# Causal mask and forget rows of an attention stage moved to rounded products on TensorE

## The chip, the cores and the metric

One core of one Trainium2 chip runs the whole program. The metric is the device time of one execution in microseconds (us), the median of several runs.

## The reference, cut to what matters

Two networks run one after the other. The change lies in the second, in the attention of its mixer, once in each of its two layers: 512 tokens, 8 heads of 64, causal, with a forget bias.

```python
def forgetting_attention(q, k, v, f_logit):
    scale = 1.0 / float(np.sqrt(dh))
    c = jnp.cumsum(jax.nn.log_sigmoid(f_logit.astype(jnp.float32)), axis=1)
    ...
    for blk in range(s // Q_BLOCK):                     # Q_BLOCK = 128
        qs, qe = blk * Q_BLOCK, (blk + 1) * Q_BLOCK
        sc = jnp.einsum('bhqd,bhkd->bhqk', qh[:, :, qs:qe], kh[:, :, :qe]) * scale
        sc = sc + (c[:, :, qs:qe, None] - c[:, :, None, :qe])
        causal = jnp.arange(qs, qe)[:, None] >= jnp.arange(qe)[None, :]
        sc = jnp.where(causal[None, None], sc, -jnp.inf)
        pr = jax.nn.softmax(sc, axis=-1)
        outs.append(jnp.einsum('bhqk,bhkd->bhqd', pr, vh[:, :, :qe]))
```

The term c[query] is the same for a whole row of the softmax, so the kernel adds only the part by key: one row of 512 values per head.

## The kernel before, in words

Every large product of the kernel is made of three products of rounded operands (type fp32r): a float32 operand is split into a high part, which is the value rounded, and a low part, the rest; high by high, high by low and low by high are summed in PSUM. `mm3` (lines 145 to 147) issues the three for one 128x128 block of weights and 512 tokens. Weights come in slabs of 128x1024 into two slots. ScalarE makes the high part of a slab (`split_hi`, line 133) when the slab that last used the slot is done; VectorE makes the low part (`split_lo`, line 138).

In the mixer of a layer, `mix_pe` writes out TensorE's order by hand. 28 slabs (queries, keys and values of each pair of heads, and gates) are cut into units of one `mm3`. The attention of the 8 heads is laid between the units as 32 steps, one for each head and block of 128 queries (step n: pair of heads n//8, head n//4 % 2, block n % 4):

- `forget(p, j)` (line 1883), once a head, 8 a layer: spreads the forget row of one head over all 128 partitions of PSUM bank 2. It is one float32 product with K = 8: a matrix of ones by `head_forget`, an 8x512 tile in which all rows but the head's are zero. VectorE makes this tile (`cm`, line 2183) by multiplying the forget sums with a column of the identity. ScalarE copies the bank to `forget_rows` (`cb`, line 2015).
- `scores(n)`: queries by keys (float32, K = 64, 128 to 512 columns, line 1900), and into the last 128 columns of the same sum the causal mask: identity by `future`, in float32 (line 1902), 32 a layer.
- VectorE adds the forget row to the scores and takes the extreme (`logits`, line 2194), ScalarE takes the exponential (line 2021), VectorE normalises (`probs`, lines 2200 and 2202), TensorE turns the result (`turn`, line 1910), ScalarE copies it, and `attend` (line 1921) multiplies with the values.

A float32 product is issued as two passes: two weight loads and two matmuls in the records. An fp32r product is one of each.

The stage begins with `dense(0)`, `dense(1)`, `forget(0, 0)`, half of `dense(2)`, `forget(0, 1)`, the other half, `scores(0)`; then the steps. `dense(2)` waits until slab 0 is taken out of its bank by `slab_out(0)` on VectorE (`evac`; queries, line 2171). VectorE's own order ahead of it is: the forget logits and their running sum (lines 2160 and 2161, each held to the one before by a chain of semaphore waits of length `FCHAIN`), `cm(0, 0)`, `slab_out(0)` (split of the next slab, then queries), four taps of a convolution (`taps`, line 2125), `slab_out(1)` (split, then keys), `cm(0, 1)`, four taps, `slab_out(2)`, four taps, `logits(0)`. The first turn waits for the first `probs`.

Right at the start of the whole kernel `act_start` on ScalarE rounds the weights of a gate (line 630), which VectorE (line 908) and then TensorE (line 1258) use.

Of the kernel before, what the change touches and what calls it, by code (L numbers as in the profile page):

```python
# [9 lines left out]
F32 = mybir.dt.float32  # L10
F32R = mybir.dt.float32r
# [40 lines left out]
HEAD_DIM_2 = 64  # L52
CONV_TAPS = 31
STEPS = 32
FCHAIN = 7

CREDIT = 2
NEG_CREDIT = 8
# [92 lines left out]
def make_layer_memory(nc, K, at):  # L151

    def put(name, shape, dtype=F32, where=None):
        nonlocal at
        size = 4 * int(np.prod(shape[1:]))
        offset = at if where is None else where
        t = nc.alloc_sbuf_tensor_at(name, shape, dtype, offset=offset)
        if where is None:
            at += -(-size // 32) * 32
        return t  # L160
    K.gains = put("gains", [128, 8 * (4 * LAYERS + 1)])
    K.cw = put("conv_taps", [128, LAYERS * 4 * CONV_TAPS])
    K.cbias = put("conv_bias", [128, LAYERS * 4])
    K.gconv = put("conv_gain", [128, LAYERS * 4])
    K.bf = put("forget_bias", [8, LAYERS])
    K.future = put("future", [128, 128])
    K.wf = put("forget_weights", [128, 8, 8])
    K.negmax = put("negmax", [128, 8])
    K.rowsum = put("rowsum", [128, 8])
    K.rowinv = put("rowinv", [128, 8])  # L170
    K.layer_x = at
    K.xgh = put("x_hi", [128, 8, 512], F32R)
    K.xgl = put("x_lo", [128, 8, 512], F32R)
    K.rstd = put("rstd", [128, 512])
    K.std = K.pb[7]
    K.sqsum = put("square_sum", [128, 512])
    K.sqtmp = put("squares", [128, 512])

    u = at
    K.layer_u = u  # L180
    K.hid_h = put("hidden_hi", [128, FT, 512], F32R)
    K.hid_l = put("hidden_lo", [128, FT, 512], F32R)
    K.sqfirst = put("first_square_sum", [128, 512], F32, u + 6144)
    K.sqw = put("weighted_squares", [128, 512], F32, u + 8192)
    K.gates = put("gates", [128, 16, 512], F32, u)
    K.mg_h = put("merged_hi", [128, 8, 512], F32R, u)
    K.mg_l = put("merged_lo", [128, 8, 512], F32R, u + 16384)
    K.glu = put("glu", [128, 4, 30 + 512], F32, u + 32768)
    K.cy = put("conv_out", [128, 4, 512], F32, u + 32768 + 8672)
    K.ao_h = put("attended_hi", [128, 4, 512], F32R, u + 49632)  # L190
    K.ao_l = put("attended_lo", [128, 4, 512], F32R, u + 57824)
    K.cv_h = put("conved_hi", [128, 4, 512], F32R, u + 66016)
    K.cv_l = put("conved_lo", [128, 4, 512], F32R, u + 74208)
    K.outt = put("out_tiles", [128, 8, 512], F32, u)
    K.crstd = put("conv_rstd", [128, 512], F32, u + 82400)
    K.cm = put("head_forget", [8, 512], F32, u + 84448)
    K.fc = put("forget_sum", [8, 512], F32, u + 86496)
    assert 86496 + 2048 <= 2 * 45056

    x = at  # L200
    K.qt = put("queries", [128, 512])
    K.kt = put("keys", [128, 512])
    K.qts = [K.qt, put("queries_odd", [128, 512], F32, u + 66016)]
    K.kts = [K.kt, put("keys_odd", [128, 512], F32, u + 68064)]
    K.vt = put("values", [128, 512])
    K.vtok = put("values_by_token", [128, 4, 128])
    K.wf_h = put("forget_hi", [128, 8, 128], F32R, x)
    K.wf_l = put("forget_lo", [128, 8, 128], F32R, x + 4096)
    K.p_h = put("embed_hi", [128, 2, 512], F32R, x)
    K.p_l = put("embed_lo", [128, 2, 512], F32R, x + 4096)  # L210
    y = at
    K.cb = [put("forget_rows0", [128, 512]), put("forget_rows1", [128, 512])]
    K.p_in = put("embed_in", [128, 2, 512], F32, y)

    z = at
    K.lg = [put("logits0", [128, 512]), put("logits1", [128, 512])]
    K.pr = [put("probs0", [128, 512]), put("probs1", [128, 512])]
    K.fx = put("forget_logits", [8, 512], F32, z)
    K.fe = put("forget_exp", [8, 512], F32, z + 2048)
    K.onerow = put("ones_row", [8, 512], F32, z + 4096)  # L220

    w = at
    K.pt = put("probs_by_key", [128, 4, 512])
    K.t1 = put("t1", [128, 512], F32, w)
    K.t2 = put("t2", [128, 512], F32, w + 2048)
    K.silu = put("silu", [128, 512], F32, w + 4096)
    K.g = put("g", [128, 512], F32, w + 6144)
    K.sig = [(K.t1, K.t2), (K.pr[0], K.pr[1])]
    K.ma = put("merge_attention", [128, 512], F32, z)
    K.mc = put("merge_convolution", [128, 512], F32, z + 2048)  # L230
    return at
# [298 lines left out]
def delta_block(K):  # L530
# [65 lines left out]
    def act_start(act):  # L596
        for dst, src in K.consts_first:
            act.dma_start(dst, src).then_inc(S.cond_in, 16)
        act.wait_ge(S.cond_in, 16 * len(K.consts_first))
        nc.scalar.activation(K.cvec[:, :, :], K.cvec[:, :, :], ACT.Silu).then_inc(S.prep_ready, 1)  # L600
        act.wait_ge(S.x_in, 32)
        for m in range(8):
            if m >= 2:
                act.wait_ge(S.ssum, 2 * (m - 1))
            nc.scalar.activation(K.ssqt[m % 2][:, 0:TOK], h[:, m, :], ACT.Square).then_inc(S.nsq_ready, 1)
            nc.scalar.activation(K.ssqt[m % 2][:, TOK:ALLT], K.ctx[:, m, :], ACT.Square).then_inc(S.nsq_ready, 1)

        def row(b):
            act.wait_ge(S.mod_row, b + 1)
            nc.scalar.activation(K.modrow[b][0:2, :], pb[b][0:2, :], ACT.Copy).then_inc(S.rows_kept, 1)  # L610
        row(0)
        row(1)
        for n, w in ((0, TOK), (1, CTX)):
            act.wait_ge(S.nsum_ready, n + 1)
            nc.scalar.activation(pb[4 + n][:, 0:w], pb[4 + n][:, 0:w], ACT.Sqrt, bias=K.eps[:, 0:1], scale=1.0 / D)\
                .then_inc(S.nstd_ready, 1)
        row(2)
        row(3)
        act.wait_ge(S.mod_ready, 3)
        for m in range(8):  # L620
            for n, (a, b) in enumerate(((0, TOK), (TOK, ALLT))):
                act.wait_ge(S.sxn_ready, 2 * m + n + 1)
                nc.scalar.activation(hnh[:, m, a:b], K.sxn[m % 2][:, a:b], ACT.Identity, bias=K.modv[:, m, n:n + 1])\
                    .then_inc(S.hnh_ready, 1)
            if m == 0:
                split_hi(act, DN_SLAB, 0, 1024)
            if m == 4:
                split_hi(act, DN_SLAB + 1, 1, 1024)
        act.wait_ge(S.const_in, 16 * K.const_count)
        nc.scalar.activation(K.wabh[:, :, :], K.wab[:, :, :], ACT.Copy).then_inc(S.prep_ready, 1)  # L630

    def act_mod_gate(act):
# [995 lines left out]
def transformer_layers(K):  # L1628
# [218 lines left out]
    def mix_pe(pe, l):  # L1847
# [27 lines left out]
                last.then_inc(S.slab_done, 1)  # L1875

        def forget(p, j):
            pe.wait_ge(S.cm_ready, 8 * l + 2 * p + j + 1)
            if j == 0:
                pe.wait_ge(S.vtok_ready, 4 * l + p + CREDIT)  # L1880
            else:
                pe.wait_ge(S.cb_ready, 8 * l + 2 * p + j)
            nc.tensor.matmul(pb[2][:, :], K.ones[0:8, :], K.cm[0:8, :], start=True, stop=True)\
                .then_inc(S.cbp_ready, 1)

        def values(p):
            pe.wait_ge(S.evac, v1 + (6 * p - 1 if p else 2) + 3)
# [5 lines left out]
        def scores(n):  # L1893
            p, j, i = n // 8, n // 4 % 2, n % 4
            if n % 8 == 0:
# [3 lines left out]
            bank = pb[3 + n % 2]  # L1899
            nc.tensor.matmul(bank[:, 0:w], K.qts[p % 2][64 * j:64 * j + 64, 128 * i:128 * i + 128],  # L1900
                             K.kts[p % 2][64 * j:64 * j + 64, 0:w], start=True, stop=False)
            nc.tensor.matmul(bank[:, w - 128:w], K.ident[:, :], K.future[:, :], start=False, stop=True)\  # L1902
                .then_inc(S.sc_ready, 1)

        def turn(n):
# [200 lines left out]
    def mix_dve(dve, l):  # L2106
# [52 lines left out]
        dve.wait_ge(S.fln_ready, l + 1)  # L2159
        chain.link(nc.vector.tensor_tensor(K.fx[R, :], K.fx[R, :], K.fe[R, :], ALU.subtract))  # L2160
        chain.link(nc.vector.tensor_tensor_scan(K.fc[R, :], K.onerow[R, :], K.fx[R, :], 0.0, ALU.mult, ALU.add))
        chain.leave(LAYERS, FCHAIN)
        hold(dve, S)

# [2 lines left out]
        def slab_out(t):  # L2167
# [8 lines left out]
                dst = K.gates[:, i, :] if kind == "g" else (K.kts[i % 2] if kind == "k" else K.vt)[:, :]  # L2176
                ins = nc.vector.tensor_tensor(dst, pb[t % 2][:, :], rstd[:, :], ALU.mult)
            ins.then_inc(S.evac, 1)

        def cm(p, j):  # L2180

            dve.wait_ge(S.cbp_ready, 8 * l + 2 * p + j + CREDIT)
            nc.vector.tensor_scalar(K.cm[0:8, :], K.fc[0:8, :], K.ident[0:8, 2 * p + j:2 * p + j + 1], None, ALU.mult)\
                .then_inc(S.cm_ready, 1)

        def logits(n):
            w = 128 * (n % 4 + 1)
# [19 lines left out]
            nc.vector.tensor_tensor(K.ao_l[:, p, :], pb[7][:, :], K.ao_h[:, p, :].bitcast(F32), ALU.subtract)\  # L2207
                .then_inc(S.ao_ready, 1)

        cm(0, 0)  # L2210
        slab_out(0)
        taps(4)
        slab_out(1)
        cm(0, 1)
        taps(4)
        slab_out(2)
        taps(4)
# [1 line left out]
        for n in range(STEPS):  # L2219
            probs(n)  # L2220
            if n + 1 < STEPS:
                logits(n + 1)
            if n % 8 in (4, 6) and n < 24:
                cm(n // 8 + 1, n % 8 // 6)
            taps(step_taps(n))
            if n % 8 == 1 and n > 8:
                attended(n // 8 - 1)
            for t in slabs_ended(n):
                slab_out(t)
# [345 lines left out]
```

## Time and profile before

| | |
|---|---|
| median of 3 runs | 3466.36 us (3465.1 to 3466.85) |
| the profiled execution's own time | 3465.55 us |
| its span in the profile | 3463.7 us |
| mean granted TensorE clock | 0.973 |
| PE busy | 3222.2 us, 93% of the span |
| DVE busy | 1793.2 us, 52% |
| ACT busy | 1118.5 us, 32% |
| the two attention stages | about 1480 to 1700 us and 2680 to 2900 us |

PE is TensorE's matmuls, PEld its weight loads, DVE VectorE, ACT ScalarE, POOL GpSimd. A matmul's record begins with its weight load, where that load isn't hidden under the matmul before, and runs on to the end of its pipeline; so records overlap, and what an instruction takes of the engine is read from the distance between starts, not from its duration. In the granted clock 1.00 is 2.4 GHz and 0.50 is 1.2 GHz.

### The profile page before, as it was taken

Reading aid. Unit: us, or ns where it says so; the run is one execution under the profiler, and the core shown is the slowest. Engines: PE = TensorE matmul, PEld = TensorE weight load, DVE = VectorE, ACT = ScalarE, POOL = GpSimd, SP = SyncE. Lnnn points to the kernel's source line nnn. Section 1 sums busy time; section 2 is a strip of 40 time slices with the busy share of each in tenths; the row PEclk is TensorE's granted clock in tenths of the full one; section 3 lists DMA queues with packets and bytes.
Section 4 is the critical chain, followed back from the end, with each engine's and each line's share of the span. In section 5 each row is a group of like instructions: output and inputs, shape, how many; then the busy total and the mean of one; then the engine's idle time right before and its main releaser. Section 6 shows DMA issues by size and latency. Waiting matters only on the chain.

```text
span 3463.7 us, 42274 instructions
## 1 busy us (share of the span) xinstructions
PE 3222.2 (93%) x14872; PEld 2538.2 (73%) x14872; DVE 1793.2 (52%) x2703; ACT 1118.5 (32%) x1578; POOL 680.6 (20%) x562
## 2 busy tenths in 40 slices
PE   5978888679999999999999999999999999999997
PEld 1768777477777888766777888778887667788885
DVE  3456666646555433477664343543335776633335
ACT  2433334224423332233433332333222334332223
POOL 0023333336442111100021111311110000211112
PEclk9989899889999999999999999999999999999998
DMA  5120201002322222221122232222322212222322
GB/s 213 43 60 6 55 13 49 14 10 71 111 91 85 97 96 93 85 67 61 62 90 91 97 102 97 80 85 96 99 91 78 64 64 67 91 91 96 102 98 74
DMA packets 96229, 271.77 MB, mean 78 GB/s; under 512 B 36400, under 2 KB 37680, under 8 KB 94768
## 3 DMA queue, kind: packets, MB, share of 16 engines
q1 hardware_dynamic: 94928, 269.00, 24.0%
q8 instruction: 74, 1.21, 0.1%
q0 software_dynamic: 320, 1.05, 0.1%
q14 instruction: 43, 0.35, 0.0%
q10 hardware_dynamic: 864, 0.16, 0.0%
HBM read 264.92 MB, written 5.24 MB: 78 GB/s over the span
## 4 chain that ended last, share of the span: by engine, by line
PE 80%; DVE 8%; ACT 3%; issue 3%; DMA 2%; POOL 2%; SPq 0%; ACTq 0%; DVEq 0%; POOLq 0%
PE bank L145 22%; PE bank L146 21%; PE bank L147 21%; PE bank L1392 2%; PE bank L1401 2%; PE bank L1900 1%; PE bank L1214 1%; PE bank L1383 1%; PE bank L1921 1%; ACT weights_hi L133 1%; DVE weights_lo L138 1%; DMA norm_gain<-n_gain 1%; DVE short_conv L963 1%; DVE rstd L1685 1%; PE bank L1902 1%
## 5 line engine op out<-in xcount | busy, mean ns | idle before, releaser
L138 DVE TENSOR_TENSOR weights_lo<-weights_raw,weights_hi 128x1024 fp32r<-128x1024 f32 (+2 forms) x428 | 608.4, 1421 | 814.3 <-ACT weights_hi L133 812.6
L145 PE MATMUL bank<-x_hi,weights_hi 128*128 128x512 f32 x2112 | 848.8, 402 | 10.8 <-DVE x_lo L1649 5.9
L146 PE MATMUL bank<-x_lo,weights_hi 128*128 128x512 f32 x2112 | 837.6, 397 | 0.0
L147 PE MATMUL bank<-x_hi,weights_lo 128*128 128x512 f32 x2112 | 837.6, 397 | 0.0
L133 ACT ACTIVATE weights_hi<-weights_raw 128x1024 fp32r<-128x1024 f32 (+2 forms) x428 | 476.1, 1112 | 758.5 <-PE bank L147 713.3
L145 PEld LDWEIGHTS bank<-x_hi,weights_hi 128*128 128x128 f32 x2112 | 398.6, 189 | 111.8 <-issue 10.4
L147 PEld LDWEIGHTS bank<-x_hi,weights_lo 128*128 128x128 f32 x2112 | 398.4, 189 | 95.8
L146 PEld LDWEIGHTS bank<-x_lo,weights_hi 128*128 128x128 f32 x2112 | 398.9, 189 | 94.2 <-issue 2.2
L1840 POOL TENSOR_TENSOR g<-silu,t 128x512 f32<-128x512 f32 x88 | 113.3, 1288 | 886.8 <-DVE t L1783 886.8
L145 PE MATMUL bank<-hidden_hi,weights_hi 128*128 128x512 f32 x704 | 278.8, 396 | 0.0
L146 PE MATMUL bank<-hidden_lo,weights_hi 128*128 128x512 f32 x704 | 278.8, 396 | 0.0
L147 PE MATMUL bank<-hidden_hi,weights_lo 128*128 128x512 f32 x704 | 278.8, 396 | 0.0
L145 PE MATMUL bank<-normed_hi,weights_hi 128*128 128x512 f32 (+1 forms) x512 | 198.7, 388 | 8.5 <-DVE normed_lo L885 6.2
L1664 POOL TENSOR_TENSOR squares<-h 128x512 f32 (+1 forms) x64 | 69.4, 1084 | 653.7 <-DVE h L1801 353.1
L146 PE MATMUL bank<-normed_lo,weights_hi 128*128 128x512 f32 (+1 forms) x512 | 190.7, 372 | 0.0
L147 PE MATMUL bank<-normed_hi,weights_lo 128*128 128x512 f32 (+1 forms) x512 | 190.2, 372 | 0.0
L1785 DVE TENSOR_TENSOR hidden_lo<-g,hidden_hi 128x512 f32 (+1 forms) x88 | 61.0, 693 | 205.0 <-ACT hidden_hi L1752 205.0
L2125 DVE SCALAR_TENSOR_TENSOR conv_out<-glu,conv_taps,conv_out 128x512 f32<-128x512 f32 x240 | 165.1, 743 | 0.0
L147 PEld LDWEIGHTS bank<-hidden_hi,weights_lo 128*128 128x128 f32 x704 | 132.4, 188 | 32.0
L145 PEld LDWEIGHTS bank<-hidden_hi,weights_hi 128*128 128x128 f32 x704 | 132.4, 188 | 31.8
L146 PEld LDWEIGHTS bank<-hidden_lo,weights_hi 128*128 128x128 f32 x704 | 132.4, 188 | 31.7
L1752 ACT ACTIVATE hidden_hi<-g 128x512 f32 (+1 forms) x88 | 55.6, 632 | 303.0 <-POOL g L1840 303.0
(354 smaller groups left out, 4414.4 us busy)
## 6 DMA issues: line engine op xcount, KB each, us to landing
weights_raw<-w_ff1in SPq DMA_DIRECT2D x90, 512.0 KB, 3.5
weights_raw<-w_ff2in SPq DMA_DIRECT2D x88, 512.0 KB, 3.5
weights_raw<-w_mix SPq DMA_DIRECT2D x72, 512.0 KB, 3.5
weights_raw<-w_ff1out SPq DMA_DIRECT2D x32, 704.0 KB, 4.1
weights_raw<-w_ff2out SPq DMA_DIRECT2D x32, 704.0 KB, 4.1
weights_raw<-w_tail SPq DMA_DIRECT2D x26, 512.0 KB, 3.5
mod_weights<-w_mod SPq DMA_DIRECT2D x6, 2048.0 KB, 18.4
weights_raw<-w_dn SPq DMA_DIRECT2D x24, 512.0 KB, 3.6
```

The costliest lines, as they stand in the source:

```text
L133: nc.scalar.activation(K.wh[:, slot, 0:cols], K.raw[:, slot, 0:cols], ACT.Copy).then_inc(S.wh_ready, 1)
L138: nc.vector.tensor_tensor(K.wl[:, slot, 0:cols], K.raw[:, slot, 0:cols], K.wh[:, slot, 0:cols].bitcast(F32), ALU.subtract).then_inc(S.raw_ ...
L145: nc.tensor.matmul(out, K.wh[:, slot, a:b], xh, start=start, stop=False)
L146: nc.tensor.matmul(out, K.wh[:, slot, a:b], xl, start=False, stop=False)
L147: return nc.tensor.matmul(out, K.wl[:, slot, a:b], xh, start=False, stop=stop)
L1392: last = nc.tensor.matmul(pb[3 + i % 2][:, 128 * q:128 * q + 128], K.bl[:, i % 2, q, :], K.dd[:, i % 3, q, :], start=True, stop=True)
L1401: last = nc.tensor.matmul(pb[5 + i % 2][:, 128 * q:128 * q + 128], K.pp[:, i % 2, q, :], K.e[:, q, i % TILES, :], start=True, stop=True)
L1664: nc.gpsimd.tensor_tensor(K.sqtmp[:, :], h[:, m, :], h[:, m, :], ALU.mult).then_inc(S.sq_made, 1)
L1752: nc.scalar.activation(hid_h[:, i, :], K.g[:, :], ACT.Copy).then_inc(S.hidh_ready, 1)
L1785: nc.vector.tensor_tensor(hid_l[:, i, :], K.g[:, :], hid_h[:, i, :].bitcast(F32), ALU.subtract).then_inc(S.hid_ready, 1)
L1840: nc.gpsimd.tensor_tensor(K.g[:, :], K.silu[:, :], K.t2[:, :], ALU.mult).then_inc(S.g_ready, 1)
L2125: nc.vector.scalar_tensor_tensor(out=K.cy[:, c, :], in0=K.glu[:, c, k:k + 512], scalar=wk, in1=K.cy[:, c, :], op0=ALU.mult, op1=ALU.add).t ...
```

## The change

1. The mask product (line 1902) takes fp32r operands. `identity_r` is a new tile with the rounded identity; `future_r` lies on `future` and is written in place. ScalarE makes both once, at the start of the kernel, ahead of line 630.
2. The forget sums are split once a layer into a high and a low part: two more instructions on VectorE behind the running sum, one of them a link of the chain (`FCHAIN` is 8). `cm`, 8 times a layer, is gone, and with it its wait for the bank and TensorE's wait for each `cm`.
3. `forget` picks a head by its stationary operand, one column of the identity repeated 128 times (a step of zero), and issues two fp32r products, for the high and the low part, in place of one float32 product.

```diff
-FCHAIN = 7
+FCHAIN = 8
...
     K.future = put("future", [128, 128])
+    K.futr = put("future_r", [128, 128], F32R, at - 512)
+    K.identr = put("identity_r", [128, 128], F32R)
...
-    K.cm = put("head_forget", [8, 512], F32, u + 84448)
+    K.fch = put("forget_sum_hi", [8, 512], F32R, u + 84448)
     K.fc = put("forget_sum", [8, 512], F32, u + 86496)
+    K.fcl = put("forget_sum_lo", [8, 512], F32R, u + 86496)
...
         act.wait_ge(S.const_in, 16 * K.const_count)
+        nc.scalar.activation(K.futr[:, :], K.future[:, :], ACT.Copy)
+        nc.scalar.activation(K.identr[:, :], K.ident[:, :], ACT.Copy)
         nc.scalar.activation(K.wabh[:, :, :], K.wab[:, :, :], ACT.Copy).then_inc(S.prep_ready, 1)
...
         def forget(p, j):
-            pe.wait_ge(S.cm_ready, 8 * l + 2 * p + j + 1)
+            pe.wait_ge(S.cm_ready, l + 1)
...
-            nc.tensor.matmul(pb[2][:, :], K.ones[0:8, :], K.cm[0:8, :], start=True, stop=True)\
-                .then_inc(S.cbp_ready, 1)
+            head = K.identr[0:8, 2 * p + j:2 * p + j + 1].to_broadcast([8, 128])
+            nc.tensor.matmul(pb[2][:, :], head, K.fch[0:8, :], start=True, stop=False)
+            nc.tensor.matmul(pb[2][:, :], head, K.fcl[0:8, :], start=False, stop=True).then_inc(S.cbp_ready, 1)
...
-            nc.tensor.matmul(bank[:, w - 128:w], K.ident[:, :], K.future[:, :], start=False, stop=True)\
+            nc.tensor.matmul(bank[:, w - 128:w], K.identr[:, :], K.futr[:, :], start=False, stop=True)\
                 .then_inc(S.sc_ready, 1)
...
         chain.link(nc.vector.tensor_tensor_scan(K.fc[R, :], K.onerow[R, :], K.fx[R, :], 0.0, ALU.mult, ALU.add))
+        chain.link(nc.vector.tensor_copy(K.fch[R, :], K.fc[R, :]))
+        nc.vector.tensor_tensor(K.fcl[R, :], K.fc[R, :], K.fch[R, :].bitcast(F32), ALU.subtract).then_inc(S.cm_ready, 1)
...
-        def cm(p, j):
-
-            dve.wait_ge(S.cbp_ready, 8 * l + 2 * p + j + CREDIT)
-            nc.vector.tensor_scalar(K.cm[0:8, :], K.fc[0:8, :], K.ident[0:8, 2 * p + j:2 * p + j + 1], None, ALU.mult)\
-                .then_inc(S.cm_ready, 1)
...
-        cm(0, 0)
         slab_out(0)
         taps(4)
         slab_out(1)
-        cm(0, 1)
...
-            if n % 8 in (4, 6) and n < 24:
-                cm(n // 8 + 1, n % 8 // 6)
```

## Rows read from the trace of the kernel before

**Rows 1.** The page: busy time of each engine, us, share and records.
```profile
PE 3222.2 (93%) x14872; PEld 2538.2 (73%) x14872; DVE 1793.2 (52%) x2703; ACT 1118.5 (32%) x1578; POOL 680.6 (20%) x562
```
**Rows 2.** The chain that ended last, by engine.
```profile
PE 80%; DVE 8%; ACT 3%; issue 3%; DMA 2%; POOL 2%; SPq 0%; ACTq 0%; DVEq 0%; POOLq 0%
```
**Rows 3.** Busy time by stretch, us: PE, PEld, DVE, ACT, POOL, clock, DMA share, GB/s.
```profile
1480.00:1700.00 220.00, 217.54 (x911) 150.20 (x909) 159.08 (x304) 73.92 (x142) 11.21 (x8) 1.00 0.19 63
...
2691.80:2695.20 3.40, 3.40 (x10) 2.62 (x9) 0.84 (x2) 0.01 (x1) 0.00 (x0) 0.50 0.03 10
```
**Rows 4.** Waits of 1440 to 1760 us: waiter, awaited, us in total, times, longest.
```profile
PE bank L1883 <- DVE head_forget L2183: 1.6, 1, 1.6
...
PE bank L145 <- DVE conved_lo L2240: 1.5, 1, 1.5
...
PE bank L1910 <- DVE probs L2202: 0.9, 1, 0.9
```
**Rows 5.** Timeline of weight loads around one mask: start, us, instruction, count.
```profile
1517.69 0.30 PEld L1902 LDWEIGHTS bank<-future,identity 128*128 128x128 f32 x2
1517.91 0.19 PEld L145 LDWEIGHTS bank<-x_hi,weights_hi 128*128 128x128 f32 x1
1518.02 0.19 PEld L146 LDWEIGHTS bank<-x_lo,weights_hi 128*128 128x128 f32 x1
```
**Rows 6.** Groups by shape, PE: busy us, mean ns of one record.
```profile
L147 PE MATMUL bank<-x_hi,weights_lo 128*128 128x512 f32 x2112 | 837.6, 397 | 0.0
...
L147 PE MATMUL bank<-normed_hi,weights_lo 128*128 128x256 f32 x128 | 36.0, 281 | 0.0
```
**Rows 7.** The same, 1480 to 1700 us.
```profile
L1900 PE MATMUL bank<-keys,queries 64*128 64x512 f32 x8 | 4.5, 642 | 0.0
...
L1900 PE MATMUL bank<-keys,queries 64*128 64x128 f32 x8 | 1.9, 323 | 0.0
```
**Rows 8.** Timeline of PE, from the first forget product.
```profile
1488.16 1.12 PE L1883 MATMUL bank<-head_forget,ones 8*128 8x512 f32 x2
1489.21 0.49 PE L145 MATMUL bank<-x_hi,weights_hi 128*128 128x512 f32 x1
...
1491.87 0.40 PE L147 MATMUL bank<-x_hi,weights_lo 128*128 128x512 f32 x1
1493.84 1.12 PE L1883 MATMUL bank<-head_forget,ones 8*128 8x512 f32 x2 [1.57 <-DVE head_forget L2183]
1494.89 0.50 PE L145 MATMUL bank<-x_hi,weights_hi 128*128 128x512 f32 x1
```
**Rows 9.** Timeline of DVE at the start of the stage.
```profile
1484.71 0.68 DVE L2160 TENSOR_TENSOR forget_logits<-forget_logits,forget_exp 8x512 f32<-8x512 f32 x1 [1.49 <-ACT forget_exp L2008]
1485.43 1.21 DVE L2161 TENSOR_TENSOR_SCAN forget_sum<-ones_row,forget_logits 8x512 f32<-8x512 f32 x1
1486.79 0.47 DVE L2183 TENSOR_SCALAR head_forget<-forget_sum,identity 8x512 f32<-8x512 f32 x1
1487.19 1.21 DVE L138 TENSOR_TENSOR weights_lo<-weights_raw,weights_hi 128x1024 fp32r<-128x1024 f32 x1
1488.33 0.67 DVE L2171 SCALAR_TENSOR_TENSOR queries<-bank,rstd 128x512 f32<-128x512 f32 x1
...
1499.14 1.22 DVE L138 TENSOR_TENSOR weights_lo<-weights_raw,weights_hi 128x1024 fp32r<-128x1024 f32 x1 [2.71 <-ACT weights_hi L133]
```
**Rows 10.** ACT line 630 and DVE line 908, near the start of the kernel.
```profile
86.42 0.40 ACT L630 ACTIVATE gate_weights_hi<-gate_weights 128x256 fp32r<-128x256 f32 x1
...
88.92 0.42 DVE L908 TENSOR_TENSOR gate_weights_lo<-gate_weights,gate_weights_hi 128x256 fp32r<-128x256 f32 x1
```
**Rows 11.** Timeline of PE: first turn of layer 1; forget product and first turn of layer 2.
```profile
1504.92 0.33 PE L1910 MATMUL bank<-identity,probs 128*128 128x128 f32 x1 [0.90 <-DVE probs L2202]
...
2690.05 1.12 PE L1883 MATMUL bank<-head_forget,ones 8*128 8x512 f32 x2 [1.57 <-DVE head_forget L2183]
...
2702.67 0.33 PE L1910 MATMUL bank<-identity,probs 128*128 128x128 f32 x1 [0.89 <-DVE probs L2202]
```

## The prediction

> **What bounds the kernel now.** I read the busy times first: TensorE is busy for 93% of the span, the next engine for 52% [rows 1]. The chain that ended last agrees: 80% of it runs over TensorE [rows 2]. Both are averages, so the stage is what counts. In the stretch of the first attention stage TensorE is busy for 217.54 of 220 us, with its clock granted in full, and VectorE for 159 us [rows 3]. The waits of that stretch tell whether TensorE is held by anyone: it is held three times for more than half a microsecond by something that bears on the change, each time once. They are `forget(0, 1)` waiting for its `cm` (1.6 us), the first turn waiting for `probs` (0.9 us), and, after the last step, the product that follows the stage, waiting for the low part of the convolution (1.5 us) [rows 4]. In all the steps between, no row puts TensorE behind another engine. So there a nanosecond taken off TensorE comes off the end, and a wait at an edge must be worked out in order of time. The second layer repeats the first.
>
> **The mask product, 64 of them.** What it costs is read from the weight loads, because they show when the array is handed on. The first load of a mask starts at 1517.69. The load of the dense product behind it starts at 1517.91, under the second pass, and the next one at 1518.02 [rows 5]. Between 1517.69 and 1517.91 lie one exposed load and one pass of 128 columns; between 1517.91 and 1518.02 lies the dense load, 0.11 us, hidden under the second pass. So a load of 128 columns takes 0.11 us, a float32 pass of 128 columns as much, and the mask holds the engine for 0.33 us. With one fp32r pass the exposed load stays (0.11). The dense load then starts together with that pass, and takes 0.11 again. The pass is shorter than the load: an fp32r stream costs (397 - 281)/256 = 0.45 ns a column [rows 6], so 0.06 us for 128. The load behind is what sets the distance, and the mask takes 0.22 us. Gain 0.11 us each, not the 0.16 that the pass alone would suggest. The bounds: nothing, if a mixed group or a narrow fp32r product brings its own cost of one more 0.11; and 0.22, if the one load that is left were hidden too. I take 0.11, since the dense loads behind it are fp32r loads and show just that time. Four of the 64, `scores(0)` and `scores(1)` of each layer, lie ahead of the first turn, which waits for `probs` anyway; their gain only lengthens that wait. The other 60 give 60 x 0.11 = 6.6 us.
>
> [...]
>
> **The forget product, 16 of them.** From its first load at 1488.16 to the next product's at 1489.21 it takes 1.05 us, and 1494.89 - 1493.84 = 1.05 again [rows 8]. It is two float32 passes of 512 columns with a load ahead and the emptying of the array behind. A float32 column costs (642 - 323)/384 = 0.83 ns [rows 7], a pass 0.425 us; an fp32r pass of 512 columns 0.232 us [rows 6]. Load and emptying are the same before and after, and the second load hides under the first pass both times. Gain 2 x (0.425 - 0.232) = 0.39 us. What no row shows is a load whose column step is zero. From below it can't beat the 0.11 us of a plain one by more than that. From above the nearest row is the same plain load; if reading one address 128 times took four times as long, two loads of 0.44 us, the second hidden for 0.23 of it, would add 0.33 + 0.21 = 0.54 us and turn the 0.39 into a loss of 0.15. I take the plain load. 12 of the 16 lie in the steps: 12 x 0.39 = 4.7 us.
>
> **The start of the stage, twice.** VectorE first. `cm(0, 0)` starts at 1486.79 and the split behind it at 1487.19, so it costs 0.40 us [rows 9]. In its place come a copy of 8x512 in the chain (I take 0.47, the record of `cm`; 0.3 to 0.55) and a subtraction of the same shape and kind as line 2160, 0.6 to 0.68 us. VectorE's queue from there on is 0.65 us late. Behind it are the split, and the queries leaving their bank, which end at 1488.33 + 0.67 = 1489.00 now and at 1489.65 then. `dense(2)` waits for that, and began its load at 1489.21. The shorter `forget(0, 0)` would let it start 0.39 us earlier; instead it starts at about 1489.75, 0.54 us later than now. This is the part that loses.
>
> Then `forget(0, 1)`. Its place in the order is 0.32 us behind the last product of the half slab, which started at 1491.87, so 1492.19; it started at 1493.84 for want of `cm` [rows 8]. Nothing on VectorE holds it any more. It waits only for ScalarE's copy of the first forget row, which the shorter product makes earlier. Half a microsecond late, it starts at 1492.73, and the half slab behind it at 1492.73 + 1.05 - 0.39 = 1493.39 in place of 1494.89. That is 1.5 us to the good. It carries through to the first turn: slab 2 is done 1.5 us earlier, ScalarE's high part follows it, and VectorE, which stands idle for 2.71 us before the split of 1499.14 [rows 9], has the room, the more so without `cm(0, 1)`; so `logits(0)` and the first turn move by 1.5 too. Two layers: 3.0 us. Bounds 2 x 1.2 and 2 x 1.8, by the copy and the subtraction.
>
> **The clock.** In layer 2 the granted clock is at 0.50, the 1.2 GHz level, from 2691.80 to 2695.20 [rows 3], right behind the wait for `cm`. From forget product to first turn layer 1 takes 1504.92 - 1493.84 = 11.08 us, layer 2 takes 2702.67 - 2690.05 = 12.62 [rows 8, 11]: the low level cost 1.5 us. Layer 1 had the same wait without the fall. With the wait gone I expect the fall gone, 1.5 us. It is the least sure term: the new wait of dense(2), about 0.95 us, stands close by, and every other short idle of the kernel, moved by some microseconds, can gain or lose a fall of the same price. I carry 1.5 us to either side.
>
> **What costs nothing.** The two roundings on ScalarE at the start, each a 128x128 copy and so less than the 0.40 us of line 630, delay line 630 by at most 0.8 us, to 87.6. VectorE reads its result at 88.92 [rows 10]: 1.3 us of cover; without it the 0.8 us would pass to line 908, and TensorE uses that only much later. The six `cm` of the steps (0.40 us each) leave VectorE, which isn't the bound there. The constants come by the DMAs they came by. The wait after the last step (1.5 us [rows 4]) hangs on the sum of squares product behind the last turn and on work that the change doesn't touch; it moves as a whole.
>
> **The sum.** 6.6 + 4.7 + 3.0 + 1.5 = 15.8 us. The profiled execution took 3465.55 us (span 3463.7 and 1.85 around it), so 3449.7. The median of the runs is 0.8 above it: 3450.5 us.
>
> **The rivals.**
> 1. The narrow fp32r product is no faster than two float32 passes, through a cost of its own at the change of type or because it is issued twice all the same; that is also the case in which the mask part doesn't do what it says. For it: no row has an fp32r product under 256 columns. Against: at 256 its column is as cheap as at 512. 15.8 - 6.6 = 9.2 us: 3457.2.
> 2. Freed TensorE runs into VectorE or ScalarE in the steps, and the 11.3 us of masks and forget products come back as waits; 4.5 us are left: 3461.9. For it: VectorE is busy for 159 of 220 us. Against: through all the steps nobody made TensorE wait but once, and VectorE loses 2.4 us a layer.
> 3. The other side: the weight load with a step of zero is slow. 32 of them, and the price stands on TensorE. It decides at eight times the plain load: 0.88 us, 0.77 more for the first load, 0.88 - 0.23 = 0.65 for the second, which hides 0.23 of itself; 16 x 1.42 = 22.7, and the kernel stands at 3473.2, 0.2% above where it is now, and above that for anything slower. For it: no row excludes it. Against: the load for 8 rows has room for no more than 0.11 us in the 1.05 us of the forget product, like that for 128 rows, so it is the columns handed over that count, and their number stays 128.
> 4. Narrow fp32r loads are quick when the array is free: the exposed load of the mask and the dense one behind it take a quarter, so a mask takes 0.03 + 0.06 = 0.09 us in place of 0.22. 60 x 0.13 = 7.8 more: 3442.7. Against it: the hidden fp32r load of 0.11 [rows 5].
>
> **How the numbers follow.** The forecast 0.78, rival 1 0.08, rival 2 0.04, rival 3 0.04 (half of it mild, ending between), rival 4 0.02, the rest for what I don't see. About 0.2%, 7 us, is what a measurement of this kernel can tell from no change. The forecast's own range is 3447.5 to 3453.5: the clock's 1.5 to both sides, the edges' 0.6, some 0.02 us on each of 76 products. Widened to rival 1 and a little below, 3446.5 to 3457.5. Faster by over 0.2% (under 3459.4): forecast, rivals 1 and 4, 0.88. Within: rival 2 and a mild rival 3, 0.08. Slower 0.04.
>
> **What would show it.** Right: the weight load of a mask stands 0.22 us ahead of the second dense load behind it; the two loads of line 1883's successor are 0.66 us from the next product's; the wait before the second forget product is gone and one of about 0.9 us stands before the `dense(2)` that follows the first; the first turn still waits, by about 1.1 us; the steps show no new wait. Wrong: a distance from mask to dense as before (rival 1), waits of the turn for `probs` in many steps (rival 2), load records of the forget product well over 0.19 us (rival 3). A fall of the clock in a place where there was none would move the time by about 1.5 us with every step of the argument intact.

## The result, and the profile after

The changed kernel takes 3448.04 us (median of 5 runs, 3445.58 to 3456.01), the kernel before beside it 3466.85 (3465.10 to 3469.58). The ratio is 0.9946, 95% interval [0.9932, 0.9961]: 18.8 us faster, 13.5 to 23.6. The forecast was 3450.5, in a range of 3446.5 to 3457.5. The profiled execution took 3445.98 us, its span is 3444.2 us, 19.5 below the span of before.

The page of the changed kernel, busy time of each engine, answers to [rows 1]. TensorE has 64 records fewer (one for each mask) and 18 us less.
```profile
PE 3204.1 (93%) x14808; PEld 2523.6 (73%) x14808; DVE 1789.6 (52%) x2691; ACT 1118.6 (32%) x1580; POOL 680.3 (20%) x562
```
**The mask**, in the timeline of weight loads (start, duration, instruction), answers to [rows 5]. Line 1908 is the mask product.
```profile
1514.58 0.29 PEld L1906 LDWEIGHTS bank<-keys,queries 64*128 64x128 f32 x2 [0.16 <-issue]
1514.99 0.19 PEld L1908 LDWEIGHTS bank<-future_r,identity_r 128*128 128x128 f32 x1
1515.10 0.19 PEld L145 LDWEIGHTS bank<-x_hi,weights_hi 128*128 128x128 f32 x1
1515.21 0.19 PEld L146 LDWEIGHTS bank<-x_lo,weights_hi 128*128 128x128 f32 x1
```
From the mask's load to the second dense load it was 0.33 us; now it is 0.22. One load each, of 0.11 us, stands between the last three starts. In 62 of the 64 masks, all but those of `scores(0)`, the distances are 0.33 before and 0.22 now. The line ahead is the load of the scores' product.

**The forget product**, the second of the first layer, in the same view, answers to [rows 8]. From its first load to the next product's it takes 1492.42 - 1491.77 = 0.65 us in place of 1.05, and its wait is gone. One load (0.11 us) and two passes (2 x 0.232) make 0.57 of it; the other 0.08 us are what the prediction calls the emptying of the array.
```profile
1491.77 0.18 PEld L1889 LDWEIGHTS bank<-forget_sum_hi,identity_r 8*128 8x128 f32 x1 [0.37 <-issue]
1491.87 0.18 PEld L1890 LDWEIGHTS bank<-forget_sum_lo,identity_r 8*128 8x128 f32 x1
1492.42 0.19 PEld L145 LDWEIGHTS bank<-x_hi,weights_hi 128*128 128x128 f32 x1 [0.36 <-issue]
```
**VectorE at the start of the stage**, its timeline, answers to [rows 9]. Before, the split of the slab began 0.40 us behind the start of `cm`, which followed the running sum (1487.19 - 1486.79); now it begins 1.06 us behind the start of the copy (CAST), which follows it (1486.86 - 1485.80).
```profile
1485.80 0.41 DVE L2168 CAST forget_sum_hi<-forget_sum 8x512 fp32r<-8x512 f32 x1
1486.25 0.68 DVE L2169 TENSOR_TENSOR forget_sum_lo<-forget_sum,forget_sum_hi 8x512 fp32r<-8x512 f32 x1
1486.86 1.20 DVE L138 TENSOR_TENSOR weights_lo<-weights_raw,weights_hi 128x1024 fp32r<-128x1024 f32 x1
1487.99 0.67 DVE L2179 SCALAR_TENSOR_TENSOR queries<-bank,rstd 128x512 f32<-128x512 f32 x1
```
**The waits of TensorE** from 1440 to 1760 us (waiter, awaited, us, times, longest) answer to [rows 4]. The wait for `head_forget` is gone. One of 0.8 us for the queries is new, the first turn waits 1.2 us in place of 0.9, and the wait behind the stage is as it was.
```profile
PE bank L145 <- DVE conved_lo L2238: 1.5, 1, 1.5
PE bank L1916 <- DVE probs L2204: 1.2, 1, 1.2
...
PE bank L145 <- DVE queries L2179: 0.8, 1, 0.8
```
**Stage by stage.** The starts of three products cut each layer into pieces that can be compared between kernels whatever happens elsewhere: the first forget product, the first turn, and the product of the sum of squares behind the last turn. From the first to the second I call the start, from the second to the third the steps. In the profiles, in us, in brackets how much of a piece had the granted clock at 0.50:

| kernel | start, layer 1 / 2 | steps, layer 1 / 2 | from there to the forget logits of layer 2 | first product to the forget logits of layer 1 |
|---|---|---|---|---|
| before | 16.77 / 18.30 (3.4) | 194.31 / 194.33 | 921.6 (10.2) | 1391.4 (150.2) |
| changed | 15.18 / 15.18 | 188.50 / 190.05 (3.4) | 919.3 (6.8) | 1390.5 (146.8) |
| changed, again | 15.19 / 15.18 | 188.51 / 188.51 | 921.9 (10.2) | 1391.7 (150.2) |
| mask alone | 16.76 / 16.77 | 192.44 (3.4) / 192.47 (3.4) | 922.3 (13.7) | 1390.7 (146.8) |
| forget rows alone | 15.18 / 15.48 | 191.94 / 191.94 | 921.9 (10.2) | 1396.3 (160.4) |
| float32 forget on a broadcast column | 15.13 / 15.13 | 190.92 / 190.93 | 922.2 (10.2) | 1390.0 (146.8) |
| split behind the queries | 12.92 / 12.92 | 188.52 / 188.51 | 921.9 (10.2) | 1391.5 (153.6) |
| no mask | 15.18 / 15.16 | 186.89 (3.4) / 185.37 | 923.4 (13.7) | 1394.3 (153.6) |
| mask 256 wide | 15.17 / 15.17 | 188.79 / 188.79 | 921.5 (10.2) | 1388.2 (140.0) |
| stored columns | 15.17 / 15.18 | 188.58 / 190.13 (3.4) | 919.2 (6.8) | 1393.7 (157.0) |
| taps late | 13.85 / 13.86 | 188.45 / 188.45 | 923.3 (13.7) | 1391.3 (150.2) |
| taps late, first forget float32 | 13.39 / 13.39 | 188.45 / 188.45 | 923.3 (13.7) | 1392.1 (163.8) |

With the split behind the queries the first forget product stands later in TensorE's order, so that start isn't comparable with the others.

The two executions of the changed kernel agree in the pieces of the stage to 0.02 us where no fall of the clock lies in them; with one a piece is 1.5 us longer (190.05 against 188.51). One piece stands out without a fall: the start of layer 2 with the forget rows alone, 0.30 us over layer 1. There ScalarE began to round a slab 0.29 us later, and the turn came later by as much; why it began later isn't shown. The last column is code that none of these kernels touches, apart from two or a few small copies on ScalarE, and it moves by 8 us, in part with the time at the low level. The whole kernel's time scatters by 10 us (3445.58 to 3456.01), so I judge single edits by the pieces.

So the change itself is worth, per layer, 16.77 - 15.18 = 1.59 us at the start and 194.31 - 188.50 = 5.81 in the steps: 14.8 us in two layers. The forecast had 14.3 for the same. The other 4.7 us between the two spans lie outside it, in code that the change doesn't touch, where the changed kernel's profile also has less time at the low level.

### The profile page after: what moved, and what is told of

Read it like the earlier page. It is cut to its first block, busy times and chain, and to the rows that moved or that the text cites. A ratio compares the mean times of both kernels' runs of the same rounds, so it can differ in the third digit from the quotient of the medians.

```text
span 3444.2 us, 42136 instructions
## 1 busy us (share of the span) xinstructions
PE 3204.1 (93%) x14808; PEld 2523.6 (73%) x14808; DVE 1789.6 (52%) x2691; ACT 1118.6 (32%) x1580; POOL 680.3 (20%) x562
## 3 DMA queue, kind: packets, MB, share of 16 engines
q0 software_dynamic: 320, 1.05, 0.1%
## 4 chain that ended last, share of the span: by engine, by line
PE 80%; DVE 8%; ACT 3%; issue 3%; DMA 2%; POOL 2%; SPq 0%; ACTq 0%; DVEq 0%; POOLq 0%
PE bank L145 22%; PE bank L147 22%; PE bank L146 22%; PE bank L1397 2%; PE bank L1406 2%; PE bank L1219 1%; PE bank L1906 1%; PE bank L1388 1%; PE bank L1927 1%; ACT weights_hi L133 1%; DMA norm_gain<-n_gain 1%; DVE short_conv L968 1%; DVE rstd L1690 1%; DVE weights_lo L138 1%; PE bank L1461 1%
```

## The experiments

**1. The mask alone.** The kernel before with only this (and the two roundings):
```diff
-            nc.tensor.matmul(bank[:, w - 128:w], K.ident[:, :], K.future[:, :], start=False, stop=True)\
+            nc.tensor.matmul(bank[:, w - 128:w], K.identr[:, :], K.futr[:, :], start=False, stop=True)\
```
Expected: 

> Only the mask product is made of rounded operands; forget rows are made as before. Theory (the load behind the narrow pass sets its price, 0.11 us gained each): 6.6 us faster than before, 3460 us, give or take 3 us of the clock's falls; from the first turn to the sum of squares product 191.0 us a layer in place of 194.3; from the first forget product to the first turn 16.8 as before, with the wait for the forget tile still there. Rival (the pass sets the price, 0.16 us): 9.6 us, 189.5. Rival (no gain in a narrow rounded product): nothing, 194.3.

Measured: 3460.22 us, ratio 0.9983 [0.9974, 0.9992]. The start is as before, 16.76. Each layer's steps had one fall of the clock; less its 1.5 us they are 190.9, on the 191.0 of the theory, 1.4 us from the rival by the pass.

**2. The forget rows alone.** The changed kernel with the float32 mask:
```diff
-            nc.tensor.matmul(bank[:, w - 128:w], K.identr[:, :], K.futr[:, :], start=False, stop=True)\
+            nc.tensor.matmul(bank[:, w - 128:w], K.ident[:, :], K.future[:, :], start=False, stop=True)\
```
Expected: 

> Only the forget rows are made in the new way, the mask product is float32. Theory: 0.39 us for each of 6 products in the steps of a layer, so 192.0 us from the first turn to the sum of squares product, and 15.2 us in place of 16.8 at the start; together 7.8 us faster than before, 3459 us, give or take 3 of the clock. Rival (the load with a step of zero is slow): less gained in the steps and weight load records over 0.19 us.

Measured: 3457.88 us, ratio 0.9975 [0.9966, 0.9984]; 191.94 us in the steps of both layers, 15.18 at the start of the first. The two parts add: 194.31 - 191.94 = 2.37 here and 194.31 - 190.92 = 3.39 for the mask (from the next run, which has no fall in it) make 5.76, and together they gave 5.81. The weight loads of the forget product take 0.18 us by their records, so the rival has nothing for it.

**3. One float32 product on a broadcast column.** The changed kernel without the split:
```diff
-            head = K.identr[0:8, 2 * p + j:2 * p + j + 1].to_broadcast([8, 128])
-            nc.tensor.matmul(pb[2][:, :], head, K.fch[0:8, :], start=True, stop=False)
-            nc.tensor.matmul(pb[2][:, :], head, K.fcl[0:8, :], start=False, stop=True).then_inc(S.cbp_ready, 1)
+            head = K.ident[0:8, 2 * p + j:2 * p + j + 1].to_broadcast([8, 128])
+            nc.tensor.matmul(pb[2][:, :], head, K.fc[0:8, :], start=True, stop=True).then_inc(S.cbp_ready, 1)
```
Expected: 

> As the changed kernel, but a head's row comes from one float32 product of the repeated identity column and the unsplit forget sums: no tile per head, no split, two float32 passes of 512 columns again. Theory (the start gains by the wait that is gone, the steps by shorter passes): at the start 15.1 to 15.2 us from the first forget product to the first turn, with no wait for the queries; in the steps 6 x 0.39 = 2.4 us a layer more than the changed kernel, 190.9; in all 4.8 us slower than the changed kernel, 3453, give or take 3. Rival (the gain of the forget part lay in taking VectorE's work away, not in the passes): as fast as the changed kernel.

Measured: 3453.65 us, ratio 0.9966 [0.9952, 0.9979]. Start 15.13, steps 190.92: both as the theory had them. This separates what the forget part does at two places. At the start the vanished wait for `cm` pays, and 15.13 against 15.18 is a balance of two more effects: without the split the third slab starts 1.05 us behind the first forget product in place of 1.51, 0.46 earlier, and the second forget product then costs 1.05 us in place of 0.65, 0.40 more.
```profile
1486.81 0.29 PEld L1889 LDWEIGHTS bank<-forget_sum,identity 8*128 8x128 f32 x2 [0.37 <-issue]
1487.86 0.19 PEld L145 LDWEIGHTS bank<-x_hi,weights_hi 128*128 128x128 f32 x1 [0.76 <-issue]
```
In the steps it is the shorter passes, 2.4 us a layer. The tile per head on VectorE (0.40 us each) doesn't matter there: the mask alone, which keeps it, has the same 190.9 us less its fall.

**4. The split moved behind the queries.**
```diff
+        slab_out(0)
         chain.link(nc.vector.tensor_copy(K.fch[R, :], K.fc[R, :]))
...
-        forget(0, 0)
-        dense(2, 0, 4)
-        forget(0, 1)
-        dense(2, 4, 8)
+        dense(2, 0, 2)
+        forget(0, 0)
+        dense(2, 2, 5)
+        forget(0, 1)
+        dense(2, 5, 8)
```
Expected: 

> As the changed kernel, but VectorE splits the forget sums after it has taken the queries from their bank, and TensorE puts the first forget product behind two units of the third slab and the second behind five. Theory (the late queries cost 0.8 us a layer): no wait for the queries, and from the forget logits' product to the first turn 77.9 us in place of 78.7; 1.6 us faster than the changed kernel, 3446.4. Rival (the first turn is set by a chain that does not start at the queries, and waits the longer): 78.7, no gain.

Measured: 3446.27 us, ratio 0.9943 [0.9929, 0.9956]; from the forget logits' product to the first turn 65.70 + 12.92 = 78.62 us, in the changed kernel 63.52 + 15.18 = 78.70. I had expected 77.9. The theory fell, at least as I had put it; that the whole time met the expected 3446.4 is luck. The waits of TensorE in this kernel, 1480 to 1510 us, show the wait for the queries shrunk, not gone:
```profile
PE bank L1916 <- DVE probs L2202: 1.2, 1, 1.2
PE bank L145 <- DVE queries L2177: 0.5, 1, 0.5
```
The late queries had a second tenant: while TensorE waited for them it also did the first forget product. Taken from there and put between dense units, that product costs its full 0.65 us, and its load stands 0.56 us behind the last dense load in place of the 0.23 between dense loads.
```profile
1488.96 0.19 PEld L145 LDWEIGHTS bank<-x_hi,weights_hi 128*128 128x128 f32 x1 [0.94 <-DVE weights_lo L138]
...
1490.01 0.19 PEld L147 LDWEIGHTS bank<-x_hi,weights_lo 128*128 128x128 f32 x1
1490.57 0.18 PEld L1889 LDWEIGHTS bank<-forget_sum_hi,identity_r 8*128 8x128 f32 x1 [0.37 <-issue]
```
Counted from the forget logits' product, the third slab starts at 64.09 us in place of 65.02 (1488.96 and 1488.78 in the two profiles), 0.93 earlier, and its last weight load stands at 71.03 in place of 71.10: 0.86 of the 0.93 us go to the product that was moved into it.

**5. No mask product** (the causal mask is left out): the scores' product ends the sum.

Expected: 

> As the changed kernel without the mask product (the causal mask is left out). Theory (the dense load behind the mask is exposed in any case, so the mask now costs one load of 0.11 us): 30 x 0.11 = 3.3 us a layer less in the steps, 185.2 us in place of 188.5, 6.6 us in all. Rival (the mask costs the whole 0.22 us between its load and the second dense load): 181.9, 13.2 us in all.

Measured: 3449.46 us, ratio 0.9947 [0.9932, 0.9962], with more time at the low level in the first network; the steps without a fall 185.37 us, 3.1 less than with the mask. The weight loads, where the mask stood, with the last load of the scores ahead:
```profile
1516.64 0.29 PEld L1906 LDWEIGHTS bank<-keys,queries 64*128 64x128 f32 x2 [0.17 <-issue]
1517.05 0.19 PEld L145 LDWEIGHTS bank<-x_hi,weights_hi 128*128 128x128 f32 x1
1517.16 0.19 PEld L146 LDWEIGHTS bank<-x_lo,weights_hi 128*128 128x128 f32 x1
```
The first dense load stands 0.11 us ahead of the second with the mask or without, and the second stands 0.52 us behind the first load of these scores, where it stood 0.63 behind it with the mask (1515.21 - 1514.58): the mask costs one more load of 0.11 us. Over 30 masks the 3.1 us are 0.105 each.

**6. A mask 256 columns wide**, zeros in the first 128:
```diff
+            m = min(w, 256)
-            nc.tensor.matmul(bank[:, w - 128:w], K.identr[:, :], K.futr[:, :], start=False, stop=True)\
+            nc.tensor.matmul(bank[:, w - m:w], K.identr[:, :], K.futw[:, 256 - m:256], start=False, stop=True)\
```
Expected: 

> As the changed kernel, but from the second block on the mask product is 256 columns wide (zeros in front of the mask), in 24 of 32 steps a layer. Theory (a load of 0.11 us hides behind the pass and sets its price; 256 columns take 0.116): 23 x 0.01 = 0.2 us a layer more, 188.7 us. Rival (the columns are paid): 23 x 0.058 = 1.3 us a layer more, 189.8.

Measured: 3454.77 us, ratio 0.9962 [0.9946, 0.9977] (its profiled execution, 3445.98, was the quickest of its kernel); the steps 188.79 us, 0.29 over the changed kernel, near the theory's 0.2 and far from the 1.3 of paid columns. Weight loads around such a mask: 0.11 and 0.12 us between the starts.
```profile
1516.28 0.19 PEld L1911 LDWEIGHTS bank<-future_wide,identity_r 128*128 128x128 f32 x1 [0.33 <-issue]
1516.39 0.19 PEld L145 LDWEIGHTS bank<-x_hi,weights_hi 128*128 128x128 f32 x1
1516.51 0.19 PEld L146 LDWEIGHTS bank<-x_lo,weights_hi 128*128 128x128 f32 x1
```
The whole times of this run and the next lie 5 to 6 us above run 8's beside them. The steps account for 0.6 and 0.2 us of it in two layers; the rest isn't explained.

**7. Stored columns for 7 of 8 heads**, the eighth broadcast:
```diff
+            head = K.heads[0:8, c, :] if c < 7 else K.identr[0:8, c:c + 1].to_broadcast([8, 128])
```
Expected: 

> As the changed kernel, but for 7 of the 8 heads the repeated identity column is stored with a step of one instead of being read with a step of zero. Theory (a load with a step of zero costs what a plain one does): the weight load records of both kinds at 0.18 us, a forget product 0.65 us from its first load to the next product's in both, the steps at 188.5 us. Rival (it costs more): the stored ones shorter than the eighth.

Measured: 3454.30 us, ratio 0.9960 [0.9945, 0.9976], again with the low level in other places; steps 188.58. Groups of weight loads by shape (busy us, mean ns): stored, then broadcast.
```profile
L1893 PEld LDWEIGHTS bank<-forget_sum_hi,head_columns 8*128 8x128 f32 x14 | 2.5, 181 | 5.1 <-issue 4.4 <-DVE forget_sum_lo L2173 0.7
...
L1893 PEld LDWEIGHTS bank<-forget_sum_hi,identity_r 8*128 8x128 f32 x2 | 0.4, 180 | 0.7 <-issue 0.7
```
A step of zero costs nothing: 181 and 180 ns by the records, and 656 and 653 ns from the product's first load to the next one's.

**8. The changed kernel once more.**

Expected: 

> The changed kernel once more. Theory (the stages' own times are fixed and the falls of the clock move between executions): 15.2 us at the start and 188.5 us in the steps of each layer where no fall lies in them, and 1.5 to 1.7 us more for each 3.4 us of the low level; the falls stand in other places than in its first profile.

Measured: 3448.99 us, ratio 0.9943 [0.9930, 0.9957]; 15.2 and 188.51 in both layers, and no fall in the steps of layer 2, where the first profile had one. Its span, 3449.8, is 5.6 above the first profile's of the same program.

**9. A version that takes out both waits at the start.** First the taps alone, then with the first forget product as one float32 product in its old place and the split behind the queries:
```diff
-        taps(4)
         logits(0)
...
-            taps(step_taps(n))
+            taps(step_taps(n) + 4 * (n == 0))
```
```diff
+            if p == j == 0:
+                nc.tensor.matmul(pb[2][:, :], K.ident[0:8, 0:1].to_broadcast([8, 128]), K.fc[0:8, :], start=True, stop=True)\
+                    .then_inc(S.cbp_ready, 1)
+                return
...
+        slab_out(0)
         chain.link(nc.vector.tensor_copy(K.fch[R, :], K.fc[R, :]))
```
Expected, the taps: 

> As the changed kernel, but the four convolution taps that VectorE lays ahead of the first logits (2.65 us) come behind the second logits. Theory (the first turn waits 1.2 us for a VectorE chain that has these taps in it): the wait is gone and the way from the forget logits' product to the first turn is 77.5 us in place of 78.7, the steps 188.5 or little more; 2.4 us faster than the changed kernel. Rival (the chain is held by ScalarE or by the slab's split, not by the taps): the wait stays.

Measured: 3448.14 us, ratio 0.9946 [0.9932, 0.9959]; from the forget logits' product to the first turn 63.52 + 13.85 = 77.37 in layer 1 and 77.36 in layer 2, the steps 188.45. The turn's wait is gone; the one for the queries, 0.8 us, stays.

Expected, both: 

> As taps_late, and the first forget product of a layer is one float32 product on the unsplit sums in its old place; VectorE splits the sums behind the queries. Theory (the first forget product lies under the wait for the queries, which is why moving it out in the reordered kernel gave nothing): the longer product (1.05 us) still ends about when the queries are out, the third slab starts 0.5 us earlier, and the way to the first turn is 77.0 us; 3.4 us faster than the changed kernel, 3445. Rival (the third slab's start carries nothing to the first turn): 77.5, as taps_late.

Measured: 3447.50 us, ratio 0.9944 [0.9930, 0.9957]; 63.51 + 13.39 = 76.90, steps 188.45. Of TensorE's waits of the start, 1470 to 1720 us, only the one behind the stage is left:
```profile
PE bank L145 <- DVE conved_lo L2243: 1.5, 1, 1.5
```
Both steps came in the size expected, 1.33 and 0.47 us a layer, but the second not quite for the reason given. In layer 1 of this version's trace the queries leave their bank at 1488.83 us, and the third slab's first load stands at 1489.68, right at the end of the product's 1.05 us:
```profile
1488.16 0.67 DVE L2180 SCALAR_TENSOR_TENSOR queries<-bank,rstd 128x512 f32<-128x512 f32 x1
...
1488.63 0.29 PEld L1890 LDWEIGHTS bank<-forget_sum,identity 8*128 8x128 f32 x2 [0.37 <-issue]
1489.68 0.19 PEld L145 LDWEIGHTS bank<-x_hi,weights_hi 128*128 128x128 f32 x1 [0.76 <-issue]
```
So the product no longer lies under a wait; it sets the slab's start itself, 0.85 us behind the queries. The slab starts 1.05 us behind the product's first load in place of 1.51, and these 0.46 us reach the first turn. In run 4 the slab started 0.93 us earlier and the turn gained 0.08, because the product had been put into the slab: what counts is when the slab ends. In the pieces this version beats the changed kernel by 3.7 us in all. The whole kernel's time can't show it (3447.50 against 3448.04 and 3448.99, each moved by falls of the clock elsewhere).

## Why the prediction was right, step by step

- **The bound.** TensorE set the steps, and nothing took the gain back: no new wait appeared in them. Rival 2 is out. At the start TensorE waits twice, 0.8 and 1.17 us, both as forecast in kind.
- **The mask, 0.11 us each.** Measured 3.39 us a layer (before against run 3) for 30 masks, 0.113 each, where the forecast had 0.11. That it is the load and not the pass that sets the price was argued from three starts; runs 5 and 6 show it. Rival 1, no gain, and rival 4, quick loads, are out; the narrow product's load takes the plain 0.11 us. The Trainium skill (TensorE: Matmul & The Clock Gate, Weight-path perf modes) has fast weight load on when the number of weights is 128 and the input type isn't FP32, with a gain in theory of four times for fp8 and none for fp32. No gain of this kind shows in the fp32r loads here.
- **The forget product, 0.39 us each.** Measured 1.05 - 0.65 = 0.40 and 2.37 us a layer for six. Rival 3 is out by run 7.
- **The start, 1.5 us a layer.** Measured 1.59. Counted from the forget logits' product, the third slab started 0.47 us later (65.02 in place of 64.55) where 0.54 was said, and its wait came out at 0.8 where 0.95 was said. Copy and subtraction took 1.06 us, as was put down for them (0.40 + 0.65), but the copy started 0.09 us sooner than `cm` had (62.04 and 62.13). The second forget product started 1.17 us earlier (1.11 was said), the half slab behind it 1.57 (1.50), and the first turn 1.57. The first turn waits 1.17 us; 1.1 was said.
- **The clock, 1.5 us.** This is the one term that was mis-stated. The fall behind the wait for `cm` went with the wait: no profile without that wait has one there. But it was no fixture of the kernel before either: with the same wait, the mask alone shows none at the start of either layer (16.76 and 16.77), so it followed that wait once in four. But the change made the first turn's wait longer, 0.9 to 1.17 us, and put the risk there. In the 12 profiles every fall inside the stage but the one of before begins 0.6 to 2.1 us behind the first turn: in 5 of the 17 layers where that wait was 1.16 us or more (one of them in the changed kernel's first profile), in none of the 3 where it was 0.9, in none of the 4 where run 9 had removed it. So the fall was moved more than removed. That it needs the longer wait is what these counts suggest, not what they prove. Elsewhere falls of the same length came and went in code that is the same in all these kernels, and in two executions of one program. The 4.7 us by which the spans differ beyond the stage's 14.8 are 0.9 before the stage, 2.3 between the layers and 1.5 at the end, where the time at the low level is shorter by 3.4, 3.4 and 1.3 us; at half speed that is about 4.1 us, and the rest isn't explained. Inside layer 2 one fall was lost and one won. The second profile gives 13.9 us between the spans. So the sum's 15.8 was right within the noise, but in its last term by luck; that term should have stood as a spread only: the sum without it, 14.3, meets what the pieces show, 14.8, and the median, 18.8 lower with an interval of 13.5 to 23.6, can't tell the two.
- **What costs nothing** did cost nothing: the six `cm` that left VectorE in the steps changed no wait, and the two roundings none near the start.

## What to carry to other kernels

Read what an instruction costs TensorE from the distance between starts of weight loads around it, and work out which of load and pass ends last after the edit: shortening a narrow pass behind which a load of 128 columns stands gains only down to that load (0.11 us here). Where an edit delays an engine that another waits for, list what already lies under that wait before moving it; here a product under the wait was free, and cost 0.86 us when moved out, so that 0.93 us of an earlier start gave 0.08. And when falls of the clock scatter the whole time by more than the edit is worth, compare the pieces between fixed products in the profiles.

## What the runs showed of the hardware

- A rounded product of 128 columns between weight loads of 128 columns takes 0.11 us, and one of 256 columns 0.12: the width is nearly free up to there.
- A stationary operand read with a step of zero loads in 180 ns by its record, a stored one in 181.
- A wait of TensorE of 1.2 us can be followed by 3.4 us at 1.2 GHz, begun 1.7 us behind the end of the wait, though the engine is busy again all through. That the wait is the cause isn't shown. Busy time and clock (before the DMA share) of the stretch behind the first turn of layer 2, which had waited 1.16 us, in the changed kernel's first profile:
```profile
2690.60:2694.00 3.40, 3.40 (x10) 2.63 (x9) 3.37 (x9) 1.06 (x3) 0.00 (x0) 0.50 0.00 0
```
The same wait in layer 1, and in both layers of the second profile, was not followed by one. The fall costs 1.5 us.
